# Handing over to the first expert: one-hot products instead of a second gather, choices of single tiles held in PSUM

## What is computed

```python
g_logits = (xt @ w_group) + b_group
g_sel = jnp.argmax(g_logits, axis=-1)
e_logits = jnp.einsum('nd,gde->nge', xt, w_router) + b_router
e_logits = jnp.take_along_axis(e_logits, g_sel[:, None, None], axis=1)[:, 0]
top_val, top_idx = lax.top_k(e_logits, MOE_TOP_K)          # 2 of the 8 experts of the group
...
h = jax.nn.silu(xb @ w_gate[e]) * (xb @ w_up[e])           # per block of 128 rows of one expert
return h @ w_down[e]
...
y = jax.ops.segment_sum(out * row_w[:, None], row_tok, num_segments=n + 1)[:n]
```

## Time and profile before

| what | us |
|---|---|
| median of 3 runs (2421.26 to 2429.83) | 2421.83 |
| the profiled execution | 2423.24 |
| its span, first to last instruction | 2421.5 |
| TensorE busy | 2316.2 (96%) |
| VectorE busy | 1805.0 (75%) |
| ScalarE busy | 1375.1 (57%) |
| GpSimd busy | 286.8 (12%) |

### The profile page before, as it was taken

The page is one execution under the profiler, slowest core; times in us unless marked ns, Lnnn a source line. Parts: engine busy times, 40 slices in busy tenths (PEclk is TensorE's granted clock), DMA queues, the critical chain, the costliest instruction groups (busy, mean ns, idle before and its releaser), DMA issues. The chain is left out here.

```text
span 2421.5 us, 34208 instructions
## 1 busy us (share of the span) xinstructions
PE 2316.2 (96%) x12916; PEld 1892.6 (78%) x12916; DVE 1805.0 (75%) x2538; ACT 1375.1 (57%) x1690; POOL 286.8 (12%) x251
## 2 busy tenths in 40 slices
PE   8999998999999999998899999998989999999996
PEld 6777886887888888886677777777878888888883
DVE  4565556688999999997555455556689999999997
ACT  3454446126777777775344444444047777777774
POOL 0000000021212112111500000000031112111104
PEclk9999999999999999999999999998989999999999
DMA  4110003328999999999211111104149999999986
GB/s 127 28 32 27 27 10 93 137 105 350 390 386 377 385 385 384 389 388 333 93 47 45 39 38 38 38 36 168 44 177 403 397 396 400 390 379 382 373 340 255
DMA packets 156078, 534.40 MB, mean 221 GB/s; under 512 B 40160, under 2 KB 80120, under 8 KB 106760
## 3 DMA queue, kind: packets, MB, share of 16 engines
q1 hardware_dynamic: 136784, 498.46, 54.4%
q0 software_dynamic: 18496, 33.60, 3.7%
q10 hardware_dynamic: 632, 0.10, 0.0%
HBM read 515.23 MB, written 50.41 MB: 234 GB/s over the span
## 5 line engine op out<-in xcount | busy, mean ns | idle before, releaser
L367 DVE TENSOR_TENSOR arena<-arena,arena 128x2048 fp32r<-128x2048 f32 (+1 forms) x458 | 956.0, 2117 | 65.2 <-ACT arena L2013 48.1
L2013 ACT CAST arena<-arena 128x2048 fp32r<-128x2048 f32 x384 | 716.4, 1918 | 150.6 <-PE psum L1732 116.2
L1732 PE MATMUL psum<-arena,arena 128*128 128x512 f32 x3072 | 734.5, 395 | 0.0
L1732 PEld LDWEIGHTS psum<-arena,arena 128*128 128x128 f32 x3072 | 570.2, 189 | 114.4 <-issue 0.4
L664 PE MATMUL psum<-arena,arena 128*128 128x512 f32 x2016 | 505.9, 401 | 6.4 <-DVE arena L367 5.6
L664 PEld LDWEIGHTS psum<-arena,arena 128*128 128x128 f32 x2016 | 369.5, 189 | 100.1 <-issue 11.4
L1743 PE MATMUL psum<-arena,arena 128*128 128x512 f32 x1536 | 359.6, 390 | 2.8 <-DVE arena L367 2.8
L1743 PEld LDWEIGHTS psum<-arena,arena 128*128 128x128 f32 x1536 | 288.1, 188 | 63.9 <-DVE arena L367 4.0
L367 DVE TENSOR_TENSOR arena<-psum,arena 128x512 fp32r<-128x512 f32 (+1 forms) x186 | 160.5, 870 | 108.7 <-ACT arena L789 55.2
L806 ACT ACTIVATE arena<-arena,arena 128x640 f32<-128x640 f32 (+4 forms) x192 | 120.0, 626 | 204.4 <-DVE arena L904 154.0
L1211 PE MATMUL psum<-arena,arena 128*128 128x512 f32 x768 | 187.0, 400 | 8.4 <-ACT arena L363 6.9
(11 more groups left out here) (189 smaller groups left out, 1776.1 us busy)
## 6 DMA issues: line engine op xcount, KB each, us to landing
arena<-in_moe_w_gate SPq DMA_DIRECT2D x128, 1024.0 KB, 8.6
arena<-in_moe_w_up SPq DMA_DIRECT2D x128, 1024.0 KB, 7.6
arena<-in_moe_w_down SPq DMA_DIRECT2D x128, 1024.0 KB, 6.9
arena<-expert_rows SPq DMA_DIRECT2D x32, 512.0 KB, 11.2
x_rows<-arena SPq DMA_DIRECT2D x24, 512.0 KB, 2.6
arena<-in_c_w_in SPq DMA_DIRECT2D x24, 512.0 KB, 4.2
arena<-x_rows SPq DMA_DIRECT2D x24, 512.0 KB, 7.9
arena<-in_x SPq DMA_DIRECT2D x16, 512.0 KB, 6.9
```

The source lines that it names most:

```text
L367: return eng.tensor_tensor(tile, src, high.bitcast(F32), ALU.subtract)
L1732: mm = pe.matmul(bank(o), cs[:, c * P:(c + 1) * P], ws[:, c * FF:(c + 1) * FF], start=(k == 0 and c == 0), stop=(k == 2 and c == CH - 1))
L2013: act.copy(w_hi[w][:, cols], self.raw[w][:, cols]).then_inc(hi_ready[w], 1)
```

## The change

Six things change in each of the two layers.

1. **Early gather.** After `lists(1)` the list of the frames of tiles 0 to 5 is complete. `list_some` turns expert 0's column of it into row numbers, and POOL gathers those rows at once, in the middle of its work on tiles 6 and 7 (`gather_some`).
2. **One-hot products.** Expert 0's columns are summed in PSUM by three rounds of eight products (`gather_here`): tile 6's rows times a one-hot matrix `own_slots[0]`, the gathered rows times the identity, tile 7's rows times `own_slots[1]`. So expert 0 waits neither for a gather of the full list nor for a transpose. `own_slot` makes a one-hot matrix from a tile's ranks.
3. **PSUM as scratch.** The choices of single tiles and the constants `iota_cols` and `down_cols` of `select(1)` and `select(3)` are held in spare PSUM banks (class `Near`).
4. **Last sum by halves.** Tile 7's residual sum and moments are made for each half of the columns, the first half two quarters before the projection's end.
5. **First gate in pieces.** `first_gate` makes gate 0's products in five runs as the columns and low parts become ready; DVE makes only half of gate 0's low part ahead of the row numbers, then expert 0's low columns.
6. **New order in the first expert.** The turn of expert 1 moves into the products of up 0; the casts and low parts of gate 1, down 0 and up 1 move behind `hid` of expert 0. Gate 1's weights are fetched as its halves come free and no longer after expert 0's gather; expert 1's gather no longer waits for expert 0's to land.

```diff
+                    def gather_here(rows, pick, first=False, halves=()):
+                        for j in range(CH):
+                            mm = pe.matmul(bank(moe.B_XT + j // 4)[:, (j % 4) * P:(j % 4 + 1) * P], rows[:, j:D:CH],
+                                           pick, start=(first and j % 4 == 0), stop=(j in halves),
+                                           skip_group_check=True)
+                            if j in halves:
+                                mm.then_inc(halves[j], 1)
...
-                    ranks(2)
-                    keep_at_work(pe, 0, 5)
-                    router(T - 1)
-                    keep_at_work(pe, 0, 3)
-                    route_logits(T - 1)
-                    lists(2)
-                    keep_at_work(pe, 0, 14)
-                    ranks(3)
+                    keep_at_work(pe, 0, 3)
+                    router(T - 1)
+                    ranks(2)
+                    keep_at_work(pe, 0, 3)
+                    route_logits(T - 1)
+                    lists(2)
+                    pe.wait_ge(own_steps, 2)
+                    gather_here(rows_all[:, T - 2, :], own_slots[0], first=True)
+                    keep_at_work(pe, 2, 3)
+                    pe.wait_ge(moe.rows_ready, 1 + 1)
+                    pe.wait_ge(early_in, 16)
+                    gather_here(early_rows, ident[:])
+                    keep_at_work(pe, 2, 2)
+                    ranks(3)
...
-                    keep_at_work(pe, 0, 3)
+                    pe.wait_ge(own_steps, 4)
+                    pe.wait_ge(ones_sent, ENTRY[3] + 2)
+                    gather_here(rows_all[:, T - 1, :], own_slots[1], halves={3: x_turned, 7: moe.xt_ready})
                     lists(3)
-                    keep_at_work(pe, 0, 10)
-                    pe.wait_ge(lists_ready, FIRST)
...
+                        if nt == 1:
+                            near = early_near if g == 2 else late_near
+                            gc, se, ca = near.gcand, near.sel, near.cand
...
-                            if nt == 1:
+                            if nt == 1 and k == E:
                                 L(dve.scalar_tensor_tensor(out=candidates[:, 0, :], in0=values[:, 0, :], scalar=top,
                                                            in1=order, op0=ALU.is_equal, op1=ALU.mult))
                             else:
...
-                    add(T - 1)
-                    norm_sum(T - 1)
-                    select(2)
-                    norm_scale(dve, T - 1, chain, root_ready, scale_ready)
-                    keep_logits(T - 1)
-                    choose(3)
-                    select(3)
+                    t = T - 1
+                    L(add_half(t, 0))
+                    moments_half(t, 0)
+                    list_some()
+                    add_half(t, 1).then_inc(added, 1)
+                    dve.wait_ge(added, t + 1)
+                    L(moments_half(t, 1))
+                    norm_spread(dve, t, chain, var_ready)
+                    own_slot(2)
+                    norm_scale(dve, t, chain, root_ready, scale_ready)
+                    select(2)
+                    keep_logits(t)
+                    choose(3)
+                    L(late_near.keep_consts(dve))
+                    own_slot(3)
+                    select(3)
                     dve.wait_ge(counted, COUNTS)
                     L(dve.tensor_copy(count_row, bank(B_COUNT)[:, 0:E]))
+                    first_split()
...
+                    def gather_some():
+                        clear_rows()
+                        pool.wait_ge(before.x1_first, 16 * (TILES - 2))
+                        pool.wait_ge(before.lists_ready, SOME)
+                        pool.wait_ge(rows_ready, 1 + 1)
+                        gather(0, plan[:, EXTRA + 1:EXTRA + 2], rows_in[0], (TILES - 2) * P)
...
+                        def up_lo():
+                            if e == 0:
+                                turn(1, 0, 1)
+                            pe.wait_ge(lo_ready[UP], 1 + 2 * (e + 1))
```

214 lines of the change are left out of this document (141 added, 73 removed).

## The result

| | median us | runs | profiled execution us | its span us |
|---|---|---|---|---|
| before | 2426.76 (2421.26 to 2432.23) | 11 | 2423.24 | 2421.5 |
| changed | 2430.76 (2427.7 to 2439.96) | 11 | 2427.7 | 2425.7 |

The changed kernel takes 1.0028 of the time before, with an interval of 1.0016 to 1.0040: 4 to 10 us slower. (That ratio is an estimate from the single runs of both, not the quotient of the two medians, which is 1.0016. The forecast was 6.3 us faster, and 2430.76 lies above its range.

A forecast was written before the change was run, and what follows sets the result against it. PE bounds the loop and DVE the hand-over from projection to experts. Savings of 1.55 + 1.6 = 3.2 us per layer, 6.3 in two, take 2423.24 to 2416.9 us profiled (median 2415.5), range 2408 to 2424.

The forecast's parts named there:

- Up to tile 7's logits: From the projection's end to tile 7's logits: the sum by halves gains between nothing and 0.8 us, taken as nothing.
- POOL: POOL's products for tile 7 start 0.85 us sooner, and the early gather ahead of them costs POOL nothing.
- Tile 7's choices: DVE's choices for tile 7: two instructions with two SBUF operands still wait for POOL; end at 537.0, saving 0.6 us.
- choices free of POOL: Rival, 0.18: two SBUF operands don't hold small instructions up; choices end at 534.1, 5.1 us per layer, 2411.5 us.
- eight take 1.9 us: Expert 0's columns on PE: eight 128x128 gather products take 1.9 us, leaving PE free at 535.5, before the choices end.
- the forecast 1.55 us: DVE after tile 7's choices: its first low part starts at 539.6, 1.55 us sooner.
- the waits of DVE: DVE in the first two experts: waits of 2.5 and 2.6 us beside 37.3 us of work, together 43.7 instead of 45.3.
- The first wait: DVE's wait for expert 1's columns: 2.5 us, if expert 1's rows are there.
- the prediction's fourth rival (the late gather): Rival, 0.09: expert 1's gather is late at its turn between up 0's products; decides from 9.3 us on; 2424 us.
- a forecast gain of 3.2 us: Per layer, to the end of `hid` of expert 1: 1.55 us from DVE's sooner start plus 1.6 from its shorter stretch.
- The new products leave no wait over 2 us by my working, so I have it at full speed: PE in the hand-over from projection to experts: no wait over 2 us, so full clock.
- The clock rival: Rival, 0.03: PE stays at the lower clock for 20 products behind the second low half; 1.5 us per layer lost, 2425.

The follow-up runs named there:

- kernel 4: The changed kernel with the logits of tiles 6 and 7 in PSUM for the choices too: 2430.40 us, 1.0022 of the kernel before.
- Kernel 11: The changed kernel with each gather's eight products taking 128 adjacent columns as weights instead of every eighth: 2422.19 us, 1.0006 of the kernel before.
- Kernels 1: The changed kernel with down 0's low part put ahead of expert 1's columns on DVE: 2424.66 us, 0.9998 of the kernel before.
- 2: The changed kernel with gate 1's casts put ahead of the copy of expert 1's columns on ACT: 2425.45 us, 1.0001 of the kernel before.
- kernel 5: The changed kernel with down 0 first on DVE and gate 1's casts first on ACT: 2419.87 us, 0.9982 of the kernel before.
- kernels 10: The changed kernel with 22 and 16 fillers on PE in its waits ahead of gate 1 and gate 2: 2428.72 us, 1.0025 of the kernel before.
- 12: The changed kernel with 12 and 9 fillers on PE in its waits ahead of gate 1 and gate 2: 2425.21 us, 1.0006 of the kernel before.
- kernel 13: The changed kernel with both orders mended, shorter front, lists ahead, and ACT's exponentials moved into expert 2's step: 2413.24 us, 0.9966 of the kernel before.

## Why the prediction was wrong

**Right.** *Up to tile 7's logits*, nothing: the choices begin at T0 + 5.9, before at T0 + 5.8. *POOL*: its products start 0.9 us sooner (T0 + 5.4 against 6.4), 0.85 was predicted, and the gather costs it nothing. *Tile 7's choices*: the two operations named as reading two SBUF operands wait until POOL's products end, none of the others is over 0.3 us, and the end at T0 + 13.0 stands against 12.8 predicted. The rule that the prediction takes from the Trainium skill ("SBUF — State Buffer", section "Who interferes with whom") agrees with the trace: kernel 4 took one SBUF operand away and the stalls went with it, 1.68 and 1.77 us down to 0.17 and 0.20. The rival "choices free of POOL" is out, as is the worth of it: kernel 4 had those free choices and gained nothing.

**Wrong, first step: "eight take 1.9 us".** They take 4.0. The price came from fillers, whose weights are adjacent columns; these weights are every eighth. So PE was free for tile 7's rank sums at T0 + 14.4 and not at 11.3, DVE waited 1.44 us for them, where PE was to have 1.5 to spare, and expert 0's columns ended with the third group at T0 + 19.5, when DVE was already through with its first low part. That low part came at T0 + 16.9 and 17.4, before at 17.0: the forecast 1.55 us are gone. Kernel 11, with products of 2.03 us, has it at T0 + 15.4, as forecast: the rest of this part of the working was right. The Trainium skill bears on it, on the page "SBUF — State Buffer", section "Door 1: The DMA port swizzle (why `[64,N]` ≈ `[32,N]`)": accesses within one line of 16 bytes go at full rate and each that crosses to a new line pays, so fp32 can be strided by 4 elements for free. Here the stride is 8, and the trace agrees with a penalty, 335 ns against 192; no run here tries a smaller stride.

**Wrong, second step: the waits of DVE.** The prediction had 2.5 and 2.6 us, 43.7 us in all to `hid` of expert 1. There were 0.95 us for expert 0's columns (not in the list), 3.91 and 3.75; from 538.10 to the end of `hid` at 584.81 it took 46.7 us, 3 more than forecast and 1.4 more than before (45.3). The first wait grew because the gather was slower: POOL issued it at 544.18 and PE turned the rows at 551.89, 7.7 us later, where 6.1 had been taken. So PE stood idle there for a DMA, 1.19 and 1.58 us, the sign of the prediction's fourth rival (the late gather), though short of the 9.3 us from which that one was to decide. The second grew by the products in its chain (copy, casts, 16 products, turn, copy): the prediction had them at 3.75 us, and they took 5.3. With the first low part 1.45 us late, 0.95 + 1.4 + 1.15 of waits too many and 0.5 less of the rest, `hid` of expert 1 ended at T0 + 63.6 in the first layer and not at 59.1: a forecast gain of 3.2 us became a loss of 1.3.

**Wrong, third step: "The new products leave no wait over 2 us by my working, so I have it at full speed".** The clock rival was put at the products behind gate 0's second low half, with a clock under 0.9 between 540 and 555 for its sign, and given 0.03; at that distance from T0 (537.05 to 552.05 here) the granted clock was 1.00. It fell later, behind PE's waits of 2.85 us for gate 1's casts, which the prediction did not have as a wait of PE at all, and 2.16 us for expert 2's columns.

**The step that weighs most: the price of the new order.** The prediction saw that down 0 "used to fill the first wait" and "now queues behind both", and that PE's lead would be lost at `hid` of expert 1. It then priced the new order as if DVE only had to get through 37.3 us of work with two waits in it. Kernels 1, 2 and 5 show what that order costs: with the same work and the same products ahead of it, only 4.5 us of low parts or 3.7 us of casts put ahead of a wait instead of behind it, H falls by 3 us a layer for each and by 5.4 for both (means over the layers; the changed kernel's over its two executions is 72.2). The forecast gain of 3.2 us a layer is there in kernel 5, which lies 3.6 and 4.3 us under before. Some 1.4 of the 5.4 us is the clock, since the waits behind which it fell are gone in kernel 5: against the layer of the changed kernel that kept the clock (70.8) the order is worth 4.0. The mispriced products are a cost beside it: kernel 11, with the order as changed, gets 2.2 to 2.5 us back. So the change's own order gives the forecast gain away, and where the clock falls behind gate 1's wait it takes 1.2 to 2.4 us more. Both orders together with adjacent weights were not run, so how far the two add up is not shown.

## What to carry to other kernels

When a change lets the bounding engine start sooner, list for each engine behind it what stands ahead of its next wait and what stands behind: work that needs nothing from that wait belongs ahead of it, and a lead is worth only what the engines behind it can keep. A price for a product is to be taken from rows with the same access pattern of the weights, not only the same size. And where a whole run scatters by more than the effect, measure a distance inside the trace between two events of the program, in several executions.

## What the runs showed of the hardware

- A weight load of 128x128 fp32 took 192 ns from adjacent columns and 335 ns from every eighth column (medians), and eight products that go through twice took 2.03 and 4.04 us (kernel 11).
- An operation of DVE on 4 to 36 elements a row with two operands in SBUF stood until POOL's product ended, 1.7 to 2.3 us in place of 0.2; with one operand in PSUM it took 0.17 and 0.20 us beside the same product (kernel 4). An operation that starts late in the product stands only for the rest of it (0.88 us).
- The granted clock fell to about 0.7 for the 16 products behind a wait of 2 to 3 us in some executions and not in others of the same kernel: 5.3 to 5.5 us or 3.9. Fillers in the wait kept those products at full clock in all eight cases, 3.9 us each (kernels 10 and 12).
- Going from silu to the exponentials on ACT and back took a table load of 1.28 us each way; with the two inside the expert loop, PE's step beside them took 19.0 us in place of 17.75 (kernel 13).
